# A hybrid decoder layer on one core: kk of the next turn a little earlier, decay sums as two float32r products, and a shorter inverse for the odd-sized group

## The reference, cut to what matters

```
g = jnp.cumsum(log_a, axis=-1)
diff = g[..., :, None] - g[..., None, :]
dec_strict = exp(where(i > j, diff, -inf));  dec_incl = exp(where(i >= j, diff, -inf))
a_kk = beta[..., :, None] * (k k^T) * dec_strict
sol = triangular_solve(a_kk, [beta*v, beta*exp(g)*k], lower, unit_diagonal)
a_qk = (q k^T) * dec_incl;  q_dec = q * exp(g);  k_dec = k * exp(g_last - g)
nu = u - w s;  o = q_dec s + a_qk nu;  s = exp(g_last) * s + k_dec^T nu      # chunk after chunk
```

## Time and profile before

| | us |
|---|---|
| median of 3 runs (3371.04 to 3372.77) | 3372.26 |
| the profiled execution | 3370.85 |
| its span, from the first to the last instruction | 3369.1 |
| busy in the span: PE | 3254.8 (97%) |
| DVE | 1354.7 (40%) |
| ACT | 913.1 (27%) |
| POOL | 820.7 (24%) |

### The profile page before, as it was taken

How to read it: one execution, slowest core, us unless ns; L and a number is a source line. 1 busy time by engine, 2 the same in 40 slices (tenths; PEclk the granted TensorE clock), 3 DMA queues, 4 the chain that set the end, 5 groups by cost and what they waited for, 6 DMA issues and landing times. The chain is left out here.

```text
span 3369.1 us, 50801 instructions
## 1 busy us (share of the span) xinstructions
PE 3254.8 (97%) x20030; PEld 3193.3 (95%) x20030; DVE 1354.7 (40%) x2258; ACT 913.1 (27%) x1379; POOL 820.7 (24%) x458
## 2 busy tenths in 40 slices
PE   8999999999999999999999999889999999999998
PEld 8999999998999999999999999779999999999997
DVE  4333333333677633433334343434314333333333
ACT  5111111112422333433444244311123111111113
POOL 2122111113222322323223232221242211111212
PEclk9999999999999999999999999889999999999999
DMA  4111111111323311212112121447212111111101
GB/s 135 44 37 50 44 44 44 44 31 41 105 87 99 105 46 56 78 51 69 58 51 76 51 84 41 143 145 266 71 46 63 50 44 44 44 44 37 45 24 54
DMA packets 275534, 226.44 MB, mean 67 GB/s; under 512 B 12171, under 2 KB 251915, under 8 KB 275441
## 3 DMA queue, kind: packets, MB, share of 16 engines
q1 hardware_dynamic: 275140, 225.08, 22.0%
q10 hardware_dynamic: 324, 0.41, 0.0%
HBM read 172.92 MB, written 52.54 MB: 67 GB/s over the span
## 5 line engine op out<-in xcount | busy, mean ns | idle before, releaser
L211 PE MATMUL ffn_bank<-ffn_h_hi,ffn_w_hi 128*128 128x368 f32 x2112 | 697.6, 330 | 6.9 <-DVE ffn_h_lo L620 6.9
L212 PE MATMUL ffn_bank<-ffn_h_lo,ffn_w_hi 128*128 128x368 f32 x2112 | 698.4, 331 | 0.0
L213 PE MATMUL ffn_bank<-ffn_h_hi,ffn_w_lo 128*128 128x368 f32 x2112 | 697.2, 330 | 0.0
L211 PE MATMUL mix_bank<-both_h_hi,mix_w_hi 128*128 128x368 f32 x1848 | 661.3, 358 | 5.1 <-DVE mix_pre L2014 3.2
L212 PE MATMUL mix_bank<-both_h_lo,mix_w_hi 128*128 128x368 f32 x1848 | 612.4, 331 | 0.0
L213 PE MATMUL mix_bank<-both_h_hi,mix_w_lo 128*128 128x368 f32 x1848 | 611.2, 331 | 0.0
L410 POOL TENSOR_TENSOR ffn_w_lo<-g_w_raw,ffn_w_hi 128x1024 fp32r<-128x1024 f32 x130 | 311.1, 2401 | 1189.8 <-ACT ffn_w_hi L406 1189.7
L819 POOL TENSOR_TENSOR mix_w_lo<-g_w_raw,mix_w_hi 128x1024 fp32r<-128x1024 f32 x77 | 193.4, 2512 | 891.5 <-ACT mix_w_hi L814 891.5
L211 PEld LDWEIGHTS ffn_bank<-ffn_h_hi,ffn_w_hi 128*128 128x128 f32 x2112 | 397.8, 188 | 8.1 <-issue 8.0
L213 PEld LDWEIGHTS ffn_bank<-ffn_h_hi,ffn_w_lo 128*128 128x128 f32 x2112 | 397.5, 188 | 0.0
L212 PEld LDWEIGHTS ffn_bank<-ffn_h_lo,ffn_w_hi 128*128 128x128 f32 x2112 | 397.3, 188 | 0.1
(11 more groups left out here) (287 smaller groups left out, 4151.7 us busy)
## 6 DMA issues: line engine op xcount, KB each, us to landing
g_w_raw<-in_w_in SPq DMA_DIRECT2D x73, 512.0 KB, 5.5
g_w_raw<-in_ffn_w_gate SPq DMA_DIRECT2D x44, 512.0 KB, 3.8
g_w_raw<-in_ffn_w_up SPq DMA_DIRECT2D x44, 512.0 KB, 3.9
g_w_raw<-in_ffn_w_down SPq DMA_DIRECT2D x44, 512.0 KB, 3.5
scratch_qkv<-mix_out SPq DMA_DIRECT2D x24, 552.0 KB, 2.8
turn_kq<-scratch_qkv SPq DMA_DIRECT2D x32, 256.0 KB, 3.5
scratch_x<-g_x SPq DMA_DIRECT2D x8, 552.0 KB, 6.9
scratch_z<-turn_z_out SPq DMA_DIRECT2D x8, 552.0 KB, 2.7
```

The source lines that it names most:

```text
L211: pe.matmul(out, w_hi, x_hi, start=first, stop=False)
L212: pe.matmul(out, w_hi, x_lo, start=False, stop=False)
L213: return pe.matmul(out, w_lo, x_hi, start=False, stop=last)
```

## The change

- The turn's order: kk of the next turn ("kk_next") comes ahead of the last dense piece of a turn, after os; before, it came after the third dense piece of its own turn. lu, q_sq, qk and vt follow after two dense pieces, then two pieces, then zero. In turn 15 os comes right after piece 33, then piece 34, kk of the first tail, piece 35, the eviction, and the roundings of y_a. The kk of turn 0 is done at the end of the projections.
- zero: DVE makes w_inv ahead of x_inv.
- Decay sums: DVE splits the small table of log decays once into a part rounded to float32r (decay_hi) and the rest; POOL makes two triangles, lu and lu_lo, both float32r; PE adds two float32r products per sum, with the triangles of ones as float32r. lu_lo lies where eg of that group lies, so POOL waits for st_ready ahead of it.
- The tails' inverse: one stage (E, Za, Zb, Zc, T), as in the full turns, takes the place of levels 1 and 2; level 3 stays a doubling (Y3, X3).
- SP issues the first weight loads of the next phase at nu of the second tail; before, it did so as the last thing in the mixer.

```diff
 turn_order():
     order.append(("load", 0))
-    dense(3)
-    order.append(("kk", 0))
+    dense(2)
     order.append(("lu", 0))
     order.append(("q_sq", 0))
-    dense(1)
     order.append(("qk", 0))
     order.append(("vt", 0))
-    dense(1)
+    dense(2)
     order.append(("zero", 0))
     ...
     order.append(("os", 0))
     dense(1)
+    order.append(("kk_next", 0))
+    dense(1)
     order.append(("out", 0))
 last_full_order():
-            order += [("dense", 35), ("evict", 8), ("ya_split", 0), ("os", 0), ("ya_split", 1)]
+            order += [("os", 0), ("dense", 34), ("kk_next", 0), ("dense", 35), ("evict", 8), ("ya_split", 0), ("ya_split", 1)]
 odd_order(g):
-    for k in range(1, TAIL_LEVELS):
-        order.append(("Y", k))
-        order.append((("dec", "eg", "sq")[k - 1], 0))
-        dense(1)
-        order.append(("X", k))
-        ...
+    order.append(("E", 1))
+    order.append(("dec", 0))
+    dense(1)
+    order.append(("Za", 1))
+    dense(1 + g)
+    order.append(("Zb", 1))
+    order.append(("eg", 0))
+    dense(1)
+    order.append(("Zc", 1))
+    order.append(("square", 0))
+    dense(1)
+    order.append(("T", 1))
+    dense(1)
+    order.append(("Y", 3))
+    order.append(("sq", 0))
+    dense(1)
+    order.append(("X", 3))
+    dense(2)
 POOL, step lu:
-                    pool.tensor_tensor(d.lu[:, :, :], over_heads(d.upto, d), tok(d, 0, t, d.n), ALU.mult).then_inc(d.on.lu_ready, 1)
+                    pool.tensor_tensor(d.lu[:, :, :], over_heads(d.upto, d), hi_tok(d, t, d.n), ALU.mult).then_inc(d.on.lu_ready, 1)
+                    pool.wait_ge(d.on.st_ready, h + 1)
+                    pool.tensor_tensor(d.lu_lo[:, :, :], over_heads(d.upto, d), tok(d, 0, t, d.n), ALU.mult) \
+                        .then_inc(d.on.lu_ready, 1)
 PE, steps dec and eg:
+            def decay_sums(d, h, name, rows, weight):
+                pe.wait_ge(d.on.lu_ready, h * 2 + 2)
+                d.norms.wait_bank(pe, d.at(h), name)
+                out = d.norms.ps(name)[0:rows, 0:HG * d.n]
+                pe.matmul(out, weight, flat(d.lu[:, :, :]), start=True, stop=False)
+                pe.matmul(out, weight, flat(d.lu_lo[:, :, :]), start=False, stop=True).then_inc(d.norms.done, 1)
 DVE, step zero:
-                    dve.tensor_tensor(d.x_inv[:, :, :], eye, d.bk[:, 0, :, :], ALU.subtract).then_inc(d.on.x_started, 1)
                     U.wait_done(dve, u, "T0")
                     dve.tensor_tensor(d.w_inv[:, :, :], eye, d.ps("T0", n, n), ALU.subtract).then_inc(U.sem("T0"), 1)
+                    dve.tensor_tensor(d.x_inv[:, :, :], eye, d.bk[:, 0, :, :], ALU.subtract).then_inc(d.on.x_started, 1)
 DVE, ahead of the last head's convolution:
+            dve.wait_ge(prep_pe, 2)
+            dve.tensor_copy(ones_r[:, :], ones)
+            dve.tensor_copy(after_r["after_tail"][0:TAIL, :], const("after_tail", TAIL))
+            dve.tensor_copy(after_r["after"][:, :], const("after"))
+            dve.tensor_copy(decay_hi[:, :, :], per_token[:, 0, :, :]).then_inc(decay_split, 1)
+            dve.wait_ge(decay_split, 1)
+            dve.tensor_tensor(per_token[:, 0, :, :], per_token[:, 0, :, :], decay_hi[:, :, :].bitcast(F32), ALU.subtract).then_inc(prep, 1)
 SP:
+                elif name == "nu" and d.g == 1:
+                    sp.wait_ge(w.lo_done, WA + WA_UNITS)
+                    slots.load_ahead(sp, ahead)
```

More of the change, by code:

```diff
@@ L956 @@
 TURN_ORDER = turn_order()
-NEXT_STEPS = ("load", "lu", "k_tok", "rate", "square", "dec", "eg", "sq", "sk", "mask", "scale")
+NEXT_STEPS = ("kk_next", "load", "lu", "k_tok", "rate", "square", "dec", "eg", "sq", "sk", "mask", "scale")
 WA = NQ + 3 * TURNS
@@ L967, in last_full_order @@
         if name == "os":
-            order += [("dense", 35), ("evict", 8), ("ya_split", 0), ("os", 0), ("ya_split", 1)]
-        elif (name, k) in (("split", 2), ("dense", 35), ("evict", 8), ("rate", 0)):
+            order += [("os", 0), ("dense", 34), ("kk_next", 0), ("dense", 35), ("evict", 8), ("ya_split", 0), ("ya_split", 1)]
+        elif (name, k) in (("split", 2), ("dense", 34), ("dense", 35), ("kk_next", 0), ("evict", 8), ("rate", 0)):
             pass
@@ L1047 @@
 _at = 0
-for _name, _width in (("upto", P), ("upto_tail", TAIL), ("after", P), ("after_tail", TAIL), ("level", (TAIL_LEVELS + STAGES) * P),
+for _name, _width in (("upto", P), ("upto_tail", TAIL), ("after", P), ("after_tail", TAIL), ("level", (2 + STAGES) * P),
                       ("segment", NSEG)):
@@ L1069, in delta_constants @@
     put("after_tail", (mt > it) & same)
-    put("level", np.concatenate([(m >> (k + 1) == i >> (k + 1)) & (m >> k & 1 == 0) & (i >> k & 1 == 1)
-                                 for k in range(TAIL_LEVELS)] +
-                                [(m >> (k + 2) == i >> (k + 2)) & (m >> k < i >> k) for k in (1, 3, 5)], 1))
+    put("level", np.concatenate([(m >> (k + w) == i >> (k + w)) & (m >> k < i >> k)
+                                 for k, w in ((0, 1), (1, 2), (3, 2), (5, 2), (3, 1))], 1))
     put("segment", seg[:, None] == np.arange(NSEG)[None, :])
@@ L1090, in mixer @@
         w_end = s.at
+        con_at = s.at
         con = s.sb("con", [P, CONST_W])
+        ones_r = s.sb("ones_r", [P, P], F32R)
+        after_r = {}
+        for name, n in (("after", P), ("after_tail", TAIL)):
+            after_r[name] = nc.alloc_sbuf_tensor_at(f"rounded_{name}", [P, n], F32R, offset=con_at + 4 * CONST_COLS[name][0])
         per_token = s.sb("per_token", [P, 4, H, NT + 1])
+        decay_hi = s.sb("decay_hi", [P, H, NT + 1], F32R)
         hp = s.sb("head_params", [2 * H, 2])
@@ L1109, in mixer @@
         v = [m.sb(f"v{p}", [P, HG, P]) for p in range(2)]
+        lu_lo = [nc.alloc_sbuf_tensor_at(f"turn_lu_lo{p}", [P, HG, P], F32R, offset=m.at + 4 * HG * P * p) for p in range(2)]
         eg = [m.sb(f"eg{p}", [P, HG, P]) for p in range(2)]
         sq = m.sb("sq", [P, 2, HG, P])
-        lu = m.sb("lu", [P, HG, P])
+        lu = m.sb("lu", [P, HG, P], F32R)
         dec = m.sb("dec", [P, HG, P])
@@ L1156, in mixer @@
         names = ["kk", "qk", "kt", "T0"]
-        for k in range(1, TAIL_LEVELS):
-            names += [f"Y{k}", f"X{k}"] + ([f"T{k}"] if k < TAIL_LEVELS - 1 else [])
+        names += ["E1", "Za1", "Zb1", "Zc1", "T1", "Y3", "X3"]
         names += ["sa", "sb", "rt", "nu", "oa", "ob"] + [f"ds{k}_{r}" for k in range(HG) for r in range(3)] + ["os"]
@@ L1179, in mixer @@
         full_on = Events(s, "")
-        full = [HeadGroup(P, g, MASKS, N, A, full_on) for g in range(2)]
+        full = [HeadGroup(P, g, STAGES, N, A, full_on) for g in range(2)]
         for g, d in enumerate(full):
@@ L1187, in mixer @@
             d.k_sum, d.k_log, d.k_norm, d.rate = [k_stat[:, r, g, :] for r in range(4)]
-            d.upto, d.after, d.z = const("upto"), const("after"), bk[:, 0, :, :]
+            d.upto, d.after, d.z, d.lu_lo = const("upto"), after_r["after"][:, :], bk[:, 0, :, :], lu_lo[g]
         def odd_view(buf, rows, *shape):
@@ L1194, in odd_view @@
                 a.rearrange("p (a b i) -> p a b i", b=shape[1], i=TAIL)
-        tails = [HeadGroup(TAIL, g, TAIL_LEVELS, NO, O, full_on) for g in range(2)]
+        tails = [HeadGroup(TAIL, g, TAIL_STAGES, NO, O, full_on) for g in range(2)]
         st_loaded, st_done = [s.sem(f"st_loaded{k}") for k in range(HG)], s.sem("st_done")
@@ L1210, in mixer @@
                 odd_view(buf[:, :, :], TAIL, HG, TAIL) for buf in (lu, dec, bdec, bmat, aqk, w_inv, y_lev, x_inv)]
[L1211 removed]
+            d.kdec, d.resid, d.nu, d.z = kdec[0:TAIL, :, :], v_tok[0:TAIL, :, :], nu[0:TAIL, :, :], d.bk[:, 0, :, :]
             d.o, d.o_sq = odd_view(o[:, :, :], P, HG, TAIL), odd_view(o_sq[:, :, :], P, HG, TAIL)
[L1213 removed]
+            d.upto, d.after = const("upto_tail", TAIL), after_r["after_tail"][0:TAIL, :]
+            d.lu_lo = odd_view(lu_lo[g][:, :, :], TAIL, HG, TAIL)
             d.qk_loaded, d.v_loaded = full[g].qk_loaded, full[g].v_loaded
@@ L1480, in _ @@
             shared(full[0], "mask", 0, 0, None, 0)
-            for j in range(1, 3):
-                w.split_lo(pool, H - 1, 3, 4 + j)
+            w.split_lo(pool, H - 1, 3, 5)
+            shared(full[0], "kk", 0, 0, None, 0)
+            w.split_lo(pool, H - 1, 3, 6)
             turns(pool, step, odd_step)
@@ L1550, in shared @@
                 if name == "dec":
-                    pe.wait_ge(d.on.lu_ready, h + 1)
-                    sums(d, h, "dec", n, d.after, d.lu[:, :, :])
+                    decay_sums(d, h, "dec", n, d.after)
                 elif name == "eg":
-                    pe.wait_ge(d.on.lu_ready, h + 1)
-                    sums(d, h, "eg", P, ones[0:n, :], d.lu[:, :, :])
+                    decay_sums(d, h, "eg", P, ones_r[0:n, :])
                 elif name in ("sq", "sk"):
@@ L1590, in shared @@
                 elif name == "Y":
-                    pe.wait_ge(d.on.bk_ready, d.masks(h) + (k + 1))
-                    U.wait_read(pe, u, f"T{k - 1}")
```

(12 more changed lines are left out.)

59 lines of the change are left out of this document (24 added, 35 removed).

## The result

The changed kernel takes 3377.64 us (median of 13 runs, 3375.1 to 3381.05), the kernel before 3372.72 beside it (13 runs): a ratio of 1.0018, 95% interval 1.0009 to 1.0026. It is slower by 5 us, 0.2%; the forecast was 3361, 11 us faster. The span of its profiled execution is 3375.2 against 3369.1.

A forecast was written before the change was run, and what follows sets the result against it. PE's instruction list was taken as the time. Terms 13.7 - 2.8 - 4.3 - 0.7 + 2.4 + 0.3 + 2.3 = 10.9 us gained, from 3370.85 to 3360.0; the median, 1.4 above, gives 3361, range 3347 to 3369.

The forecast's parts named there:

- The rest of the reordering is free: In the turns: os keeps its wait of about 0.3, masks and dec come many pieces after their inputs; no loss.
- Sums: Decay sums on PE: two float32r products take 0.46 instead of 0.86 us per 512 columns; 13.7 us gained in all.
- E2: In odd turns (1 to 13) E2 waits for ACT's copy of w_inv, so a shorter dec only lengthens it: 2.8 lost.
- Turn starts: T0's wait goes; new waits at vt (1.45 even, 0.47 odd) and E1 (0.75 even, 0.66 odd): 4.3 us lost.
- The lock: DVE's two-input SBUF products and POOL's wait out each other's whole instruction, so "out" starts at 6.9 even, 5.87 odd.
- Turn 0: POOL's masks, split and both lu lock DVE's convolution products, so E1 comes later: 0.7 us lost; without lock 2.0 gained.
- Odd-sized groups: Waits of os and T0 come back at kt and E1; still 2.4 us gained, 0.3 in the second group.
- After the mixer: The next phase starts earlier with its weights loaded; 2.3 us gained (bounds 1 and 4).
- The clock rival: Two close waits at turn starts act like one and lower PE's clock, 1.7 us in each of 15 turns: 3386; chance 0.05.

The follow-up runs named there:

- experiment 1: Changed kernel with SP issuing the q, k and v loads for the next even turn before it waits for "out" of the odd turn: 3361.31 us (0.997).
- Experiment 6: The kernel of experiment 4 with the weight split that stood before T1 put behind it: 3333.33 us (0.9887).
- experiment 5: Changed kernel with decay sums as before, one POOL product of lu and one float32 sum: 3383.34 us (1.0036).
- experiment 8: Changed kernel with the next phase's first weight loads back at the end of the mixer: 3382.37 us (1.0032).
- Experiment 2: Changed kernel with the old order of the turn (kk back in its own turn), everything else as changed: 3366.22 us (0.9983).
- experiment 4: Changed kernel with the step "out" ahead of the last dense piece of a turn instead of behind it: 3341.3 us (0.9908).

## Why the prediction was wrong, point by point

- **The step that failed: "The rest of the reordering is free".** The forecast followed vt, E1, masks and POOL's queue, but not SP's, past which kk and a dense piece were moved. It put k_tok's wait for its load at nothing, without a reason. Its own count, carried on along SP, gives the wait: "out" ends at 6.9 + 0.67 = 7.57; before, the load followed 1.41 after (1407.11 to 1408.52); PE is past E1 (10.0) and ks at 10.0 + 0.89 + 0.89 = 11.8. With the data 4.66 after the load, at 13.64, 1.8 per even turn are missing; the 4.66 is known only from the trace after, but the 4.28 of turn 6 before would give 1.5. Measured were 1.64 to 2.10. Seven of them with 0.16 of restart are 13.7. By turn 15 the forecast stood at -12.8 + 2.8 + 4.3 + 0.7 = -5.0, the trace at +8.6: 13.6 apart. That the two agree is luck: E1 came out cheaper, turn 0, the sums and the restarts dearer, and these cancel. What shows the size is experiment 1, which takes this wait alone away and gains 13.7 by the merge.
- **Sums: right.** From the last small product to the dense matmul, 1423.02 to 1424.38 is 1.36, before 1418.84 to 1420.58 1.74: 0.38 each instead of 0.40. The first of the two stands 0.32 from what follows, not the 0.23 forecast, and the second 0.23; that the saving is met all the same is because the group ahead of the float32 sum took 0.07 longer too (0.88 instead of 0.81).
- **E2: right.** 1.18 to 1.56, the 0.38 that the sum became shorter. Experiment 6 shows the bound named there, ACT's list.
- **Turn starts: T0 and vt right, E1 too dear.** T0 has no idle time, vt waits 1.32 even and 0.35 odd (forecast 1.3 and 0.3). E1 waits 0.25 with 0.16 of restart, 0.41, where 0.75 and 0.66 were put: "out" met only the end of lu_lo (1.09 instead of 1.3). This is 4.4 in the change's favour; not counted were slower groups behind a wait (E1 takes 0.99 to the next group instead of 0.89), some 1.5 in all.
- **The lock: right in kind.** The Trainium skill, "SBUF — State Buffer", section "SBUF: two separate sides", has VectorE's two-input instructions and GpSimd's SBUF readers exclude each other; the traces agree, with 1.78 instead of 0.75 for "out", 1.15 instead of 0.69 for the sum and 8.08 instead of 6.25 for the convolution. It was not what made the change slow: by experiment 5, one POOL product fewer leaves k_tok's wait as it is.
- **Turn 0: undersized.** Forecast 0.7; from k_tok of turn 0 to ds it took 1128.16 to 1214.72, 86.56, before 1128.75 to 1213.40, 84.65, though the turn's own sum is shorter. The convolution under the lock made E1 wait 6.19 and the stores of q, k, v late, so k_tok waits 1.25 there too; neither this nor the clock was in the term. Timeline of PE:

```profile
1168.76 2.07 PE L1607 MATMUL mix_a_bank<-turn_w_inv,turn_bk 128*128 128x128 f32 x8 [6.19 <-DVE turn_w_inv L1999]
1170.62 1.92 PE L1652 MATMUL mix_a_bank<-turn_state,turn_kq 128*128 128x128 f32 x8
```

  The two groups take 2.07 and 1.92 where 1.05 is usual: the clock is at half, for 6.8 us instead of 3.4.
- **Odd-sized groups: half.** kt and E1 came where forecast (8.6 late, at 2139.50 and 2148.57; minus 8.6 that is 2130.9 and 2140.0, forecast 2130.6 and 2140.3), and os and T0 no longer wait. But dec then waits 1.04 for lu_lo, which was not counted. From ds of turn 15 to the first product for the states: 61.9 instead of 63.1, 1.2 gained instead of 2.4.
- **After the mixer: right.** 2.26 instead of 2.3, and experiment 8 gives it back.
- **The clock rival** was priced rightly (1.7 a fall) and did not decide here: no fall in turns 1 to 15. Its bound, some wait between 1.86 and 3.48 from which the clock falls, does not show: it fell after 1.83 in one kernel, and not after 2.10 in another (last section). Experiment 2 shows that it was nearer than 0.05 said.

## What to carry to other kernels

When work is moved earlier, walk every engine's list that it is moved past, the DMA issuer's too: a load that stands behind a store in one issuer's list is as late as the result stored, and a room of 0.3 us does not show as a wait in the trace before. Where several waits appear at once, look for one chain that they share; here one step put a piece earlier (experiment 4) removed three waits, 36 us, while mending one wait at a time gave 16.

## What was not expected of the hardware

After a wait of 2.15 us the clock fell in four of seven turns that look alike, always every second one (1, 5, 9, 13); after 1.19 in none, and in the changed kernel it stayed full even after 2.10 (k_tok of turn 14). With float32 sums it fell twice, after k_tok's waits of 1.83 and 1.89, at 1300 and at 1915. PE, then windows of that kernel:

```profile
1298.93 0.65 PE L1584 MATMUL mix_n_bank<-g_ident,turn_kq 128*128 128x128 f32 x4 [1.83 <-DMA turn_kq<-scratch_qkv]
...
1297.00:1300.00 3.00, 1.17 (x9) 1.07 (x9) 1.65 (x3) 0.00 (x0) 0.57 (x1) 1.00 1.10 307
1300.00:1303.00 3.00, 3.00 (x14) 3.00 (x13) 0.84 (x2) 2.51 (x10) 0.00 (x0) 0.56 1.19 296
```

So the length of one wait alone does not settle it; what does is left open. In these kernels a wait of some 2 us is at times followed by a loss of 1.7.
